# Half-width products in a gated-recurrence kernel: pairs of 64 keys by 64 queries, one in each half of TensorE's columns

## The chip, the cores and the metric

The kernel runs on one core of a Trainium2 chip. The metric is the device time of one execution in microseconds (us), lower is better. TensorE (PE) multiplies, VectorE (DVE) and ScalarE (ACT) work elementwise, GpSimd (POOL) does some elementwise work here and issues a few DMAs, SyncE (SP) issues most DMAs. A product on TensorE is two records in a trace: the load of the stationary operand (LDWEIGHTS, listed as engine PEld) and the matmul that streams the moving operand past it (MATMUL, listed as PE).

## The reference, cut to what matters

Two blocks follow each other. The first has a gated linear recurrence over 16 heads; this is what the change touches:

```python
def step(S, inp):                        # one chunk of 64 positions
    qc, kc, vc, gc = inp
    b = jnp.cumsum(gc, axis=-2)
    decay = jnp.exp(jnp.where(causal, b[..., :, None, :] - b[..., None, :, :], -jnp.inf))
    scores = jnp.einsum('bhtc,bhtsc,bhsc->bhts', qc, decay, kc)
    o = einsum('bhts,bhsv->bhtv', scores, vc) + einsum('bhtc,bhcv->bhtv', qc * jnp.exp(b), S)
    ...
```

It runs forward and backward over 256 context and 512 latent positions, head size 128, and its input is a projection of the normalised tokens to five streams a head (query, two gates, value, output gate). A Fourier mixer and a second block (two feed-forward layers and a token mixer) follow; nothing in them changes. All of it is in float32.

## The kernel before

**Weights.** Every large product is made as three (high by high, high by low, low by high) of operands cut into two parts of type fp32r; they are recorded under the helper `three` at L489. SyncE brings weights in blocks of 128 by 1024 into two buffers (`w_raw`), ACT makes `w_hi` (L1060), DVE makes `w_lo` (L1603).

**Heads.** `pe_head(i, j)` is TensorE's program of one trip: the projections (`project`) of head i, and between them the recurrence of head j = i - 1. It is written out once for the first head, as a loop over 15 trips, and once for the last head, where the place of the projections is taken by the start of the output product (`begin_output`). The order inside a trip is written by hand, in three rows that begin

```python
project(0, "a"); project(0, "b"); diagonal(); level(0)
project(1, "a"); level(1); turn_v_context(); project(1, "b"); level(2)
project(1, "c"); level(3); project(2, "a"); level(4); project(2, "b"); level(5)
project(2, "c"); level(6); project(3, "a"); turn_k(0); ...
```

**Scores by levels.** The scores of the 512 latent positions are needed only inside tiles of 128 (`tile(t)`, four tiles, `TT`); between tiles the recurrence carries a state. Inside a tile they come from a tree with 7 levels: at level l a block of 2^l keys meets the sibling block of 2^l queries. `K` and `Q` hold keys and queries of both directions; `merge(l)` on DVE (L1825) multiplies them by the decays of that level, in place; ACT copies the keys of the level in order of position to `K_now` (`weave`, L1215); TensorE multiplies them with the queries, which `woven` picks from the two directions' halves of `Q` by an access pattern of runs of 2^l (L663). `diagonal` (L650) multiplies the summed keys `ksum` with `q_st` for the pairs of a position with itself. Each of these eight steps makes four float32 products of 128 keys by 128 queries, contraction 128, into one bank of `ps` (bank 4 or 5), and of each product DVE takes by mask the places that the level owns (`place`, COPY_PREDICATED at L1804) into `ST`. At levels 0 to 5 and on the diagonal these places all lie in the two 64 by 64 squares on the tile's diagonal, at level 6 in the two squares off it.

**What starts what.** TensorE waits with `dve(l)` for the queries of level l, with `k_woven` for its keys, and with `gates_ready` for `ksum`; DVE waits for TensorE's products through `pe_scan`. After level 1 come two transposes (L642), after the levels transposes of `K` (L676), products of keys and values (L685), the output (L695 to L697) and the norm (L704). At the program's start, before the heads, `ada_raw` is multiplied with a stationary operand of only two columns, `csil` (L546); in between stands the mean of L528, with a stationary operand of 128 columns; then come 16 transposes of two rows (L554).

Of the kernel before, what the change touches and what calls it, by code (L numbers as in the profile page):

```python
# [31 lines left out]
P = 128  # L32
# [30 lines left out]
LEVELS = 7  # L63
BLK = KD * P
BF = 258
HALF_T = T // 2
FOLD = TT // 2


_sizes = [("c", 2 * KD), ("ada_b0", 16), ("gate_b", 16), ("ada_b1", 16), ("norm_g0", KD), ("norm_g1", KD),  # L70
# [71 lines left out]
def woven(t, at, size, n, first):  # L142

    wide = t.shape[2]
    step = n + (wide if first == 0 else -wide)
    return bass.AP(t, at + first * wide, [[2 * wide, P], [2 * n, size // (2 * n)], [step, 2], [1, n]])
# [22 lines left out]
def program(nc, wts, ada_in, gate_in, x_in, ctx_in, meta_in, vec_in, mask_in, ident_in, dft_in, chan_in, out):  # L171
    nblocks = wts.shape[0]
    with ExitStack() as top:
# [42 lines left out]
        q_st = h.take("q_st", [P, T])  # L216
# [4 lines left out]
        Q = h.take("Q", [P, 2, T])  # L221
        K = h.take("K", [P, 2, TA])
        K_now = h.take("K_now", [P, 2, T])
        ksum = h.take("ksum", [P, T])
# [17 lines left out]
        g_hi, g_lo = f.take("g_hi", [P, KD, T], F32R), f.take("g_lo", [P, KD, T], F32R)  # L242
        F_hi = f.take("F_hi", [P, FOLD, T], F32R)
        F_lo = f.take("F_lo", [P, FOLD, T], F32R)
        C_hi = f.take("C_hi", [P, 2, 2, 2, P], F32R)
# [7 lines left out]
        fgain, fgain_sq = q.take("fgain", [P, KD]), q.take("fgain_sq", [P, KD])  # L253
        F_raw, C_raw = f.take("F_raw", [P, FOLD, T]), f.take("C_raw", [P, 2, 2, 2, P])
        h_now, h_fold = f.take("h_now", [P, T]), f.take("h_fold", [P, T])
# [34 lines left out]
        ps = top.enter_context(nc.psum_tensor("ps", [P, 8, T], F32))  # L290
# [156 lines left out]
        def _(pool):  # L447
# [26 lines left out]
            pool.wait_ge(y_cut, HEADS)  # L474
            pool.dma_start(F_raw[:], dft_in[:, 0:FOLD]).then_inc(dft_in_s, 16)
            pool.dma_start(C_raw[:], chan_in).then_inc(chan_in_s, 16)
# [5 lines left out]
        def _(pe):  # L482
            st = Stream()

            def three(outs, whi, wlo, xhi, xlo, start, stop):

                for n, (w, x) in enumerate(((whi, xhi), (whi, xlo), (wlo, xhi))):
                    for o, xp in zip(outs, x):
                        last = nc.tensor.matmul(o, w, xp, start=start and n == 0,  # L489
                                                stop=stop and n == 2)  # L490
                return last
# [7 lines left out]
            def tiles(s, outs, xs, ks, start, stop, first=0):  # L499

                for n, k in enumerate(ks):
                    c = slice((first + n) * P, (first + n + 1) * P)
                    last = three(outs, w_hi[:, s, c], w_lo[:, s, c], *xs(k),
                                 start=start and n == 0, stop=stop and n == len(ks) - 1)
                return last
# [4 lines left out]
            def halved(hi, lo):  # L510
                return lambda k: ([hi[:, k, 0:HALF], hi[:, k, HALF:TM]],
                                  [lo[:, k, 0:HALF], lo[:, k, HALF:TM]])

            def bank2(b):
                return [ps[:, b, 0:HALF], ps[:, b + 1, 0:HALF]]
# [15 lines left out]
            def tile_cols(t):  # L531
                return slice(t * P, (t + 1) * P)
# [8 lines left out]
            for n, (raw_, a, b_) in enumerate(ADA_LOADS):  # L541
                pe.wait_ge(ada_loaded[n], 16)
                for k in range(KD):
                    if n == 1 and k == KD - 2:
                        mean(N0, T, st_sum[:, 0])
                    last = nc.tensor.matmul(ps[0:2, n], csil[:, k], raw_[:, :, k * P:(k + 1) * P],  # L546
                                            start=k == 0, stop=k == KD - 1)
# [5 lines left out]
            for m_ in range(16):  # L553
                last = nc.tensor.transpose(ps[:, 7, 2 * m_:2 * m_ + 2], ada_row[:, m_ // 4, tile_cols(m_ % 4)],  # L554
                                           ident[0:2, 0:2])
# [4 lines left out]
            def tile(t):  # L560
                return slice(t * P, (t + 1) * P)
# [8 lines left out]
            def pe_head(i, j):  # L570
# [49 lines left out]
                def dve(n):  # L620
                    pe.wait_ge(dve_scan, j * DVE_SCAN + n)
# [15 lines left out]
                def turn_v_context():  # L637
# [4 lines left out]
                        last = nc.tensor.transpose(ps[:, 6, tile(t)], v_st[:, tile(t)], ident[:])  # L642
                    last.then_inc(pe_scan, 1)

                def diagonal():
                    if j is None:
                        return
                    pe.wait_ge(gates_ready, j + 1)
                    for t in range(TT):
                        last = nc.tensor.matmul(ps[:, 4, tile(t)], ksum[:, tile(t)], q_st[:, tile(t)],  # L650
                                                start=True, stop=True)
                    last.then_inc(pe_scan, 1)

                def level(l):
                    if j is None:
                        return
                    if l == 0:
                        pe.wait_ge(act_scan, j * ACT_SCAN + 7)
                    else:
                        dve(l)  # L660
                    pe.wait_ge(k_woven, j * LEVELS + (l + 1))
                    for t in range(TT):
                        last = nc.tensor.matmul(ps[:, 5 - l % 2, tile(t)], K_now[:, l % 2, tile(t)],  # L663
                                                woven(Q, t * P, P, 2 ** l, 1), start=True, stop=True)
                    last.then_inc(pe_scan, 1)

                def steps(g_):
# [32 lines left out]
                def norm():  # L700
# [3 lines left out]
                    nc.tensor.matmul(ps[:, 5], ones_h[:], osq[:], start=True, stop=True).then_inc(pe_scan, 1)  # L704
# [4 lines that stand above are left out]
                project(2, "c"); level(6); project(3, "a"); turn_k(0); project(3, "b"); outer(0)  # L709
                turn_k(1); project(3, "c"); outer(1); turn_k(2); project(4, "a"); outer(2)  # L710
# [4 lines left out]

            st.enter(0, 6)
            pe_head(0, None)
            st.leave(1)
            with hinted(pe, 0, HEADS - 1) as j:
                st.enter(j, 6)  # L720
                pe_head(j + 1, j)
            st.leave(HEADS - 1)
            st.enter(0, 2 * EARLY)
            pe_head(None, HEADS - 1)
            st.leave(1)
            pe.wait_ge(kept_s, EARLY)
            for n in range(LATE):
                t = HEADS - LATE + n
                pe.wait_ge(y_cut, t + 1)
                for k in range(EARLY):  # L730
                    last = three([ps[:, k]], kept_hi[:, k, n * P:(n + 1) * P], kept_lo[:, k, n * P:(n + 1) * P],
                                 [y_hi[:, t]], [y_lo[:, t]], False, n == LATE - 1)
# [44 lines left out]
            def over_tokens(c):  # L777
# [4 lines left out]
                for t in range(TT):  # L782
                    part, m_ = divmod(t, FOLD)
                    o, at = ((ps[:, 6, 0:BF], slice(0, BF)), (ps[:, 7, 0:HALF_T], slice(HALF_T, T)))[part]
                    last = three([o], t_hi[:, tile(t)], t_lo[:, tile(t)],
                                 [F_hi[:, m_, at]], [F_lo[:, m_, at]], m_ == 0, m_ == FOLD - 1)
                last.then_inc(pe_ft, 1)
# [177 lines left out]
            with hinted(pe, 0, KD // 2) as i:  # L965
                st.enter(i, 14)
                for k in range(14):
# [13 lines left out]
                    for m_ in range(2):  # L981
                        last = tiles(s, bank2(4 + 2 * m_), halved(xr_hi, xr_lo), range(2), True, True, 2 * m_)
# [610 lines left out]
        def _(dve):  # L1593
            st = Stream()
            own = Own(dve, own_s["dve"])
            v = nc.vector
# [66 lines left out]
            v.memset(eps[:], EPS)  # L1663
            v.memset(tiny[:], 2.0 ** -100)
            v.memset(eps_sq[:], EPS * EPS)
            v.memset(zero[:], 0.0).then_inc(consts_set, 1)
            dve.wait_ge(vec_in_s, 16)
            lb = vec[:, VEC["lb"]:VEC["lb"] + 4 * HEADS].rearrange("p (n c) -> p n c", n=2)
# [945 lines left out]
```

## Time and profile before

| | us |
|---|---|
| median of 3 runs | 2518.79 (2518.48 to 2519.62) |
| profiled execution, its own time | 2521.25 |
| span of its trace, first to last instruction | 2518.5 |
| TensorE matmul busy | 2461.1 (98%) |
| TensorE weight load busy | 2147.0 (85%) |
| VectorE busy | 1633.3 (65%) |
| ScalarE busy | 993.6 (39%) |
| GpSimd busy | 120.3 (5%) |

The mean granted clock of TensorE is 0.992 of full speed. Busy shares add up over stages that have different limits. A matmul's recorded duration reaches beyond the moment at which the next one starts, so what one costs in a row of its kind is the distance between starts, or its share of a piece in the chain of work that ended last.

### The profile page before, as it was taken

How to read it: one execution, taken by the hardware profiler on the slowest of the kernel's cores; microseconds unless marked ns; L12 is line 12 of the kernel's file. 1: busy time of each engine (PE TensorE's matmuls, PEld its weight loads, DVE VectorE, ACT ScalarE, POOL GpSimd, SP SyncE). 2: the span in 40 equal slices, each digit the busy share in tenths (PEclk: the TensorE clock that was granted, in tenths of full speed). 3: DMA queues.
4: the chain of work that ended last, by engine and by line, in shares of the span. 5: the costliest groups of instructions: out<-in, count | busy, mean ns of one | idle time of the engine just before them, and what ended most of it. 6: DMA issues, size and time to landing. Idle time of an engine off the chain costs nothing.

```text
span 2518.5 us, 40380 instructions
## 1 busy us (share of the span) xinstructions
PE 2461.1 (98%) x14398; PEld 2147.0 (85%) x14398; DVE 1633.3 (65%) x2378; ACT 993.6 (39%) x1338; POOL 120.3 (5%) x138
## 2 busy tenths in 40 slices
PE   7999999999999998999999999989999999999998
PEld 2888888888888886888899999979999878888886
DVE  7567777777777775445555343468999975444346
ACT  4334444444444433333345222235455554322223
POOL 0011211111111100000000000000000000000000
PEclk9999999999999998999999999999999999999999
DMA  6212212122121232222222222222222222222222
GB/s 239 78 64 75 75 67 75 58 76 82 67 67 64 78 126 75 83 76 83 85 92 91 88 88 92 92 84 92 100 97 94 100 84 97 95 92 92 99 92 100
DMA packets 61983, 223.90 MB, mean 89 GB/s; under 512 B 6736, under 2 KB 8784, under 8 KB 61552
## 3 DMA queue, kind: packets, MB, share of 16 engines
q1 hardware_dynamic: 58992, 211.08, 24.7%
q0 software_dynamic: 2944, 12.19, 1.4%
q8 instruction: 29, 0.48, 0.1%
q14 instruction: 18, 0.15, 0.0%
HBM read 221.15 MB, written 2.10 MB: 89 GB/s over the span
## 4 chain that ended last, share of the span: by engine, by line
PE 93%; DVE 4%; ACT 1%; issue 1%; DMA 1%; ACTq 0%; DVEq 0%; SPq 0%
PE ps L489 81%; PE ps L663 4%; PE ps L685 1%; PE ps L546 1%; DMA ada_raw<-in_ada_weights_dram 1%; PE ps L676 1%; PE ps L704 1%; PE ps L650 1%; PE ps L695 1%; PE ps L696 1%; PE ps L697 1%; ACT w_hi L1060 1%; DVE w_lo L1603 1%; PE ps L633 0%; DVE n_sq L1622 0%
## 5 line engine op out<-in xcount | busy, mean ns | idle before, releaser
L1060 ACT ACTIVATE w_hi<-w_raw 128x1024 fp32r<-128x1024 f32 (+1 forms) x360 | 377.8, 1049 | 922.5 <-PE ps L489 913.7
L1603 DVE TENSOR_TENSOR w_lo<-w_raw,w_hi 128x1024 fp32r<-128x1024 f32 (+1 forms) x360 | 435.3, 1209 | 214.4 <-ACT w_hi L1060 212.2
L489 PE MATMUL ps<-n_hi,w_hi 128*128 128x512 f32 (+1 forms) x992 | 320.5, 355 | 11.9 <-DVE n_lo L1630 8.5
L489 PE MATMUL ps<-n_lo,w_hi 128*128 128x512 f32 (+1 forms) x992 | 319.6, 354 | 0.0
L489 PE MATMUL ps<-n_hi,w_lo 128*128 128x512 f32 (+1 forms) x992 | 318.0, 352 | 0.0
L489 PE MATMUL ps<-h_hi,w_hi 128*128 128x512 f32 x640 | 266.5, 416 | 4.8 <-DVE h_lo L1735 3.1
L489 PE MATMUL ps<-h_hi,w_lo 128*128 128x512 f32 x640 | 251.2, 393 | 0.0
L489 PE MATMUL ps<-h_lo,w_hi 128*128 128x512 f32 x640 | 250.4, 391 | 0.0
L489 PEld LDWEIGHTS ps<-n_hi,w_hi 128*128 128x128 f32 x992 | 174.5, 189 | 45.4 <-issue 11.0
L489 PEld LDWEIGHTS ps<-n_hi,w_lo 128*128 128x128 f32 x992 | 174.6, 189 | 25.9
L489 PEld LDWEIGHTS ps<-n_lo,w_hi 128*128 128x128 f32 x992 | 174.4, 189 | 26.1 <-issue 0.2
L489 PE MATMUL ps<-y_lo,w_hi 128*128 128x512 f32 x504 | 179.1, 397 | 6.6 <-DVE y_lo L1630 6.6
L489 PEld LDWEIGHTS ps<-h_hi,w_hi 128*128 128x128 f32 x640 | 121.0, 189 | 32.8 <-issue 10.0
L489 PE MATMUL ps<-hid_hi,w_hi 128*128 128x264 f32 (+2 forms) x540 | 143.4, 318 | 0.7 <-DVE w_lo L1603 0.7
L489 PE MATMUL ps<-xg_hi,w_hi 128*128 128x264 f32 x704 | 143.9, 285 | 0.0
L489 PE MATMUL ps<-xg_lo,w_hi 128*128 128x264 f32 x704 | 143.8, 285 | 0.0
L489 PE MATMUL ps<-xg_hi,w_lo 128*128 128x264 f32 x704 | 143.6, 285 | 0.0
L489 PE MATMUL ps<-hid_lo,w_hi 128*128 128x264 f32 (+2 forms) x540 | 143.4, 319 | 0.0
L489 PEld LDWEIGHTS ps<-h_hi,w_lo 128*128 128x128 f32 x640 | 120.4, 188 | 26.8
L489 PE MATMUL ps<-hid_hi,w_lo 128*128 128x264 f32 (+2 forms) x540 | 142.9, 318 | 0.0
L489 PEld LDWEIGHTS ps<-h_lo,w_hi 128*128 128x128 f32 x640 | 121.3, 190 | 22.1
L1215 ACT ACTIVATE K_now<-K 128x512 f32<-128x512 f32 x112 | 75.4, 673 | 154.5 <-DVE K L1825 138.4
(367 smaller groups left out, 4963.8 us busy)
## 6 DMA issues: line engine op xcount, KB each, us to landing
w_raw<-in_weights_dram SPq DMA_DIRECT2D x376, 512.0 KB, 3.3
ada_raw<-in_ada_weights_dram SPq DMA_DIRECT2D x4, 2048.0 KB, 22.4
gate_raw<-in_gate_weights_dram POOLq DMA_DIRECT2D x16, 512.0 KB, 3.6
x<-in_x_dram SPq DMA_DIRECT2D x1, 2048.0 KB, 14.6
x<-in_x_dram POOLq DMA_DIRECT2D x1, 2048.0 KB, 9.9
out_dram<-fin SPq DMA_DIRECT2D x16, 128.0 KB, 1.9
xc<-in_ctx_dram SPq DMA_DIRECT2D x1, 1024.0 KB, 21.2
masks<-in_masks_dram POOLq DMA_DIRECT2D x1, 512.0 KB, 4.8
```

Of the source, the lines that this page charges most:

```text
L489: last = nc.tensor.matmul(o, w, xp, start=start and n == 0, stop=stop and n == 2)
L546: last = nc.tensor.matmul(ps[0:2, n], csil[:, k], raw_[:, :, k * P:(k + 1) * P], start=k == 0, stop=k == KD - 1)
L650: last = nc.tensor.matmul(ps[:, 4, tile(t)], ksum[:, tile(t)], q_st[:, tile(t)], start=True, stop=True)
L663: last = nc.tensor.matmul(ps[:, 5 - l % 2, tile(t)], K_now[:, l % 2, tile(t)], woven(Q, t * P, P, 2 ** l, 1), start=True, stop=True)
L676: last = nc.tensor.transpose(ps[:, 6, tile(x)], K[:, d, tile(ORDER[d][n])], ident[:])
L685: last = nc.tensor.matmul(ps[:, 4 + g_ % 2, tile(x)], KT[:, x], V[:, ORDER[d][n]], start=True, stop=True)
L695: nc.tensor.matmul(o, V[:, CT + t], ST[:, t], start=True, stop=False)
L696: nc.tensor.matmul(o, states[:, 1 + t, 0], Q[:, 0, tile(t)], start=False, stop=False)
L697: last = nc.tensor.matmul(o, states[:, 4 - t, 1], Q[:, 1, tile(t)], start=False, stop=True)
L1060: run(w_hi[:, s, 0:n], w_raw[:, s, 0:n], ACT.Copy).then_inc(hi_ready[s], 1)
L1215: run(K_now[:, l % 2], woven(K, TC, T, 2 ** l, 0), ACT.Copy).then_inc(k_woven, 1)
L1603: tt(w_lo[:, s, 0:n], w_raw[:, s, 0:n], w_hi[:, s, 0:n].bitcast(F32), ALU.subtract).then_inc(lo_ready[s], 1)
```

## The change

A product of 128 keys by 128 queries becomes two of 64 by 64. The keys of a half tile are the stationary operand (64 columns), and the result goes to partitions 0 to 63 of `ps` for the first half of the keys and to 64 to 127 for the second, so each product stands in one half of the array's columns. On the diagonal and at levels 0 to 5 the queries are those of the same half; at level 6 those of the other half, which lie in one direction's part of `Q` and need no weaving. The squares of the bank that are not written any more are never taken by a mask, but are still read; the two banks are set to zero once at the start.

```diff
+HALF_TILE = P // 2
...
+                def half_tiles(t):
+                    return [slice(t * P + x * HALF_TILE, t * P + (x + 1) * HALF_TILE) for x in range(2)]
+
                 def diagonal():
                     if j is None:
                         return
                     pe.wait_ge(gates_ready, j + 1)
                     for t in range(TT):
-                        last = nc.tensor.matmul(ps[:, 4, tile(t)], ksum[:, tile(t)], q_st[:, tile(t)],
-                                                start=True, stop=True)
+                        for x, c in enumerate(half_tiles(t)):
+                            last = nc.tensor.matmul(ps[x * HALF_TILE:(x + 1) * HALF_TILE, 4, c], ksum[:, c], q_st[:, c],
+                                                    start=True, stop=True)
                     last.then_inc(pe_scan, 1)
 
                 def level(l):
...
                     for t in range(TT):
-                        last = nc.tensor.matmul(ps[:, 5 - l % 2, tile(t)], K_now[:, l % 2, tile(t)],
-                                                woven(Q, t * P, P, 2 ** l, 1), start=True, stop=True)
+                        cs = half_tiles(t)
+                        for x, keys in enumerate(cs):
+
+                            at = cs[1 - x] if l == LEVELS - 1 else keys
+                            queries = Q[:, x, at] if l == LEVELS - 1 else woven(Q, at.start, HALF_TILE, 2 ** l, 1)
+                            last = nc.tensor.matmul(ps[x * HALF_TILE:(x + 1) * HALF_TILE, 5 - l % 2, at],
+                                                    K_now[:, l % 2, keys], queries, start=True, stop=True)
                     last.then_inc(pe_scan, 1)
...
             v.memset(eps_sq[:], EPS * EPS)
+            v.memset(ps[:, 4:6], 0.0)
             v.memset(zero[:], 0.0).then_inc(consts_set, 1)
```

Waits and signals stay as they are. On TensorE, in the loop over the heads, this stood from the diagonal through level 1 before (output by keys and queries; a product here is one instruction, which the trace shows as two loads and two matmuls):

```order
L489 MATMUL ps<-h_hi,w_lo 128x512
L650 MATMUL ps<-q_st,ksum 128x128 x4
L658 ISA
L661 REGISTER_ALU
L663 MATMUL ps<-Q,K_now 128x128 x4
L572 REGISTER_ALU
L489 MATMUL ps<-h_hi,w_hi 128x512
...
L663 MATMUL ps<-Q,K_now 128x128 x4
L624 ISA
L642 MATMUL ps<-ident,v_st 128x128 x2
```

And this stands there now:

```order
L490 MATMUL ps<-h_hi,w_lo 128x512
L657 MATMUL ps<-q_st,ksum 64x64 x8
L665 ISA
L668 REGISTER_ALU
L675 MATMUL ps<-Q,K_now 64x64 x8
L573 REGISTER_ALU
L490 MATMUL ps<-h_hi,w_hi 128x512
...
L675 MATMUL ps<-Q,K_now 64x64 x8
L625 ISA
L643 MATMUL ps<-ident,v_st 128x128 x2
```

Nothing has moved: each run of four products of 128 by 128 has become a run of eight of 64 by 64, between neighbours of full width. Levels 2 to 6 each stand alone between two projections in the same way. On DVE, this is the start of the program before:

```order
L1665 MEMSET eps_sq 128x1
L1666 MEMSET zero 128x1
L1669 TENSOR_TENSOR lbt<-vec 128x32
L1670 TENSOR_TENSOR lbt<-vec,lbt 128x64
L1672 TENSOR_SCALAR rgc<-vec 128x8
```

and now:

```order
L1677 MEMSET eps_sq 128x1
L1678 MEMSET ps 128x1024
L1679 MEMSET zero 128x1
L1682 TENSOR_TENSOR lbt<-vec 128x32
L1683 TENSOR_TENSOR lbt<-vec,lbt 128x64
```

One instruction, the zeroing of the two banks, has come in ahead of the signal `consts_set`.

## Rows read from the trace of the kernel before

**Rows 1.** Page, part 1: busy us, share of the span, instructions.

```profile
PE 2461.1 (98%) x14398; PEld 2147.0 (85%) x14398; DVE 1633.3 (65%) x2378; ACT 993.6 (39%) x1338; POOL 120.3 (5%) x138
```

**Rows 2.** Windows: busy us of each engine in one trip of the heads.

```profile
core 0: us, PE busy (x) PEld busy (x) DVE busy (x) ACT busy (x) POOL busy (x), PEclk, DMA share, GB/s
252.59:304.55 51.96, 51.96 (x324) 46.11 (x323) 39.51 (x63) 22.97 (x35) 7.39 (x9) 1.00 0.21 71
```

**Rows 3.** Chain that ended last, in order: start, us, work; one trip.

```profile
304.71 0.89 PE ps L650 x8
305.60 1.33 PE ps L663 x8
...
309.68 1.12 PE ps L663 x8
...
313.76 0.89 PE ps L663 x8
```

**Rows 4.** The same chain: level 1 in the second and the last head.

```profile
153.92 0.96 PE ps L663 x8
881.20 0.96 PE ps L663 x8
```

**Rows 5.** Timeline around level 3: start, us, engine, line, work.

```profile
317.25 0.28 PE L489 MATMUL ps<-hc_hi,w_lo 128*128 128x256 f32 x1
317.25 0.98 PEld L663 LDWEIGHTS ps<-Q,K_now 128*128 128x128 f32 x8
317.37 1.06 PE L663 MATMUL ps<-Q,K_now 128*128 128x128 f32 x8
```

**Rows 6.** Line L663, all of it: duration ns, min/median/max.

```profile
L663 PEld LDWEIGHTS ps<-Q,K_now x896: 186/192/198, 97.8 to 900.1; 128*128 128x128 f32 x180
L663 PE MATMUL ps<-Q,K_now x896: 270/275/383, 97.9 to 900.3; 128*128 128x128 f32 x180
```

**Rows 7.** Timeline of the start: two-column (L546) and full-width (L528) products.

```profile
26.27 0.59 PE L546 MATMUL ps<-ada_raw,csil 128*2 128x512 f32 x1
26.79 0.70 PE L528 MATMUL ps<-st_sum,ones_d 128*128 128x512 f32 x1
26.79 0.30 PEld L528 LDWEIGHTS ps<-st_sum,ones_d 128*128 128x128 f32 x2 [0.86 <-issue]
27.32 0.59 PE L528 MATMUL ps<-st_sum,ones_d 128*128 128x512 f32 x1
27.85 0.59 PE L546 MATMUL ps<-ada_raw,csil 128*2 128x512 f32 x1
30.28 13.89 PE L546 MATMUL ps<-ada_raw,csil 128*2 128x512 f32 x32
```

**Rows 8.** The 16 transposes of two rows: durations ns of the loads; timeline.

```profile
L554 PEld LDWEIGHTS ps<-ident,ada_row x16: 133/137/141, 44.9 to 45.9; 2*128 2x128 f32 x16
...
44.91 1.08 PEld L554 LDWEIGHTS ps<-ident,ada_row 2*128 2x128 f32 x16 [1.67 <-issue]
44.95 1.14 PE L554 MATMUL ps<-ident,ada_row 2*128 2x2 f32 x16 [0.77 <-ACT ada_row L1113]
```

**Rows 9.** Timeline ahead of level 1: DVE, then level 1's first load.

```profile
304.25 1.22 DVE L1603 TENSOR_TENSOR w_lo<-w_raw,w_hi 128x1024 fp32r<-128x1024 f32 x1
305.74 1.87 DVE L1825 TENSOR_TENSOR K<-K,f_st 128x768 f32<-128x768 f32 x1 [0.27 <-PE ps L650]
...
308.40 1.03 DVE L1825 TENSOR_TENSOR Q<-Q,f_st 128x512 f32<-128x512 f32 x1
309.56 1.02 PEld L663 LDWEIGHTS ps<-Q,K_now 128*128 128x128 f32 x8 [0.31 <-issue]
```

**Rows 10.** Timeline of the program's start on DVE and ahead of TensorE.

```profile
2.88 0.17 DVE L1662 MEMSET ones_h<- 128x128 f32 x1
11.60 2.72 PE L546 MATMUL ps<-ada_raw,csil 128*2 128x512 f32 x3 [11.60 <-DMA ada_raw<-in_ada_weights_dram]
17.07 0.43 DVE L1617 COPY st_sum<-st_tmp 128x512 f32<-128x512 f32 x1 [6.99 <-ACT st_tmp L1087]
```

## The prediction

> **What bounds the kernel now.** The page first: TensorE is busy 98% of the span, DVE 65% [rows 1]. The windows of one trip of the heads say it more sharply: in a trip of 51.96 us TensorE is busy for all 51.96, at full granted clock, DVE for 39.51 [rows 2]. So in the heads, where all of the change lies, a microsecond of TensorE's time is a microsecond of the kernel, as long as DVE keeps up. The chain of work that ended last prices each piece: the diagonal 0.89 us, level 0 1.33, level 1 1.12, any other level 0.89 [rows 3]. In the 16 heads there are 80 pieces of 0.89 from levels 2 to 6. Level 1 takes 1.12 (1.11 to 1.14) in the 13 heads from the third to the fifteenth, and 0.96 in the other three [rows 3, 4].
>
> What is in 0.89 us? Four products are eight passes, each a load of 128 columns and a stream of 128 queries. The matmuls start (1.06 - 0.275)/7 = 0.112 us apart, and the loads (0.98 - 0.19)/7 = 0.113 [rows 5, 6]. So a pass costs 0.111 (0.89/8), and the loads alone would fill the time as well as the streams do: each load lies under the stream before it. Level 0 costs 1.33/8 = 0.167 a pass; its queries alternate between the two halves of `Q` at every element.
>
> **What the change does to a run of products.** The passes of a diagonal or a level go from 8 to 16, each with half the columns to load and half the queries to stream. If cost follows columns, a pass falls from 0.111 to 0.056 and a run stays at 16 x 0.056 = 0.89; level 0 stays at 1.33. Halving the columns of both operands saves a factor of four in array work, but twice the passes take back a factor of two, and the other factor comes only if the two halves of the array work at the same time. The trace of before has no such pair. The least that a load with its matmul takes in it, back to back, is in the 16 transposes of two rows and two streamed columns: (1.08 - 0.14)/15 = 0.063 for the loads and (1.14 - 0.19)/15 = 0.063 for the matmuls [rows 8]. There hardly anything is streamed. I bound a half-width pass from below by 0.030 (two halves in full parallel, half of 0.056, rounded up) and from above by 0.063, and take 0.060 for the likeliest case: halves one after the other at 0.056, plus a little, towards the one row with such short work. A run then costs 0.96 instead of 0.89, so +0.07.
>
> The diagonal and levels 1 to 6 are 7 x 16 = 112 runs: 112 x 0.07 = +7.8 us (0 to +13.4 with 0.056 to 0.063). Level 0: +0.04 in 16 heads, +0.6.
>
> The Trainium skill, "TensorEngine Tiling (Array Packing)", section Key Properties, states that tiles operate independently and that different tiles can load and multiply in parallel; by it alone a pass would be near 0.030 and a run near 0.48. No row of this trace shows two tiles at work together, so it makes the second rival below and not the sum.
>
> **What it adds at the edges of a run.** This is the larger term. The trace shows TensorE changing between a narrow stationary operand and a full one, at the start of the program. Products with two stationary columns follow each other at (13.89 - 0.59)/31 = 0.429 us. From the last of them to the first full-width product it is 26.79 - 26.27 = 0.52 instead, so 0.09 more; and the full-width load starts only then, at 26.79, not under the stream before, so its 0.11 is exposed too: the next matmul follows after 27.32 - 26.79 = 0.53 = 0.43 + 0.10. Back to two columns it is again 27.85 - 27.32 = 0.53 instead of 0.43: 0.10 more, with a load too short to see [rows 7]. The second such place, around 29.65, shows the same gaps. So TensorE runs empty before it changes between a narrow and a full operand, and the first load after the change is not covered. In the heads no width changes today, and every first load lies under the stream before it [rows 5].
>
> In the changed kernel every run is fenced by full-width work on both sides. Diagonal and level 0 adjoin and make one narrow stretch, levels 1 to 6 one each: 7 stretches a head, 112 in all. Entering costs 0.09 and an exposed load of 64 columns, 0.056; leaving costs 0.09 and an exposed load of 128 columns, 0.11. That is 0.35 us a stretch, 112 x 0.35 = +39.2 us. From below: nothing, if 64 columns do not count as another shape of the array. From above: the tail of a matmul beyond its stream, 0.275 - 0.11 = 0.16 [rows 6], in place of each 0.09, so 0.49 a stretch and +55 us.
>
> The Trainium skill, same page and section, says that changing the tiling mode, not just the tile, drains TensorE. By that rule both edges of every stretch pay and the two halves inside one do not; the trace agrees for two columns against 128, with the 0.09 and 0.10 above.
>
> **What goes away.** Level 1 waits for its queries: DVE ends them at 308.40 + 1.03 = 309.43, and the load starts at 309.56 [rows 9]. That wait is the 1.12 - 0.89 = 0.23 in 13 heads. With a diagonal and level 0 that take 0.07 + 0.04 + 0.35 = 0.46 longer, TensorE comes late enough to find the queries there, though DVE's start also waits for the diagonal and slips by some 0.2 (entering plus 0.07). The wait mostly goes: 13 x 0.23 = -3.0 us.
>
> **What costs nothing.** The new MEMSET of 1024 columns. The 128-column one takes 0.17 with its fixed part, so this one takes at most 8 x 0.17 = 1.4 us, at about 3 us on DVE. TensorE's first work waits for a DMA until 11.60, and DVE later sits idle 6.99 us before 17.07 [rows 10]; both cover it. Uncovered it would be 1.4 us. DMAs, waits and signals are as before, and DVE, with 12 us to spare in a trip, follows a slower TensorE.
>
> **Sum.** +39.2 + 7.8 + 0.6 - 3.0 = +44.6 us. The profiled execution took 2521.25, so 2565.9 for its like; against the median of the runs, 2518.79 + 44.6 = **2563** us, 1.8% slower. A difference of 0.2% (5 us) is about what a measurement of this kernel can tell from none.
>
> **Rivals.**
>
> 1. *Slower by the edges, as above.* For it: both edges are in the trace, and loads fill a run today. Own range 2545 to 2580: the edges at 0.28 to 0.40 and the pass at 0.056 to 0.063. Chance 0.60. With the full tail at the edges instead it is 2518.8 + 55 + 5 = 2579 or more; chance 0.07.
>
> 2. *The halves work in parallel, and the edges are paid* (the other side). A pass averages 0.030, a run 0.48, so levels 1 to 6 save 0.41 each and pay 0.35: -0.06 x 96 = -6 us. Diagonal and level 0 together go from 2.22 to about 0.48 + 0.70 + 0.35 = 1.53, but most of that is not gained: level 1's queries are ready only 3.7 us after DVE starts on `K`, DVE starts when the diagonal is done, and it cannot start before 304.25 + 1.22 = 305.47, 0.27 ahead of today [rows 9]. So -0.25 x 16 = -4 us, and the wait at level 1 grows. 2509 us. It decides as soon as an average pass falls below (0.89 - 0.35)/16 = 0.034 us. For it: nothing forbids it in the trace, and the placing in two halves asks for it. Against: in the heads' float32 products a load starts no sooner than 0.11 after the load before it [rows 5], so one path that serves both halves in turn is enough to undo the gain. Chance 0.17.
>
> 3. *Parallel halves and free edges*: 96 x -0.41 = -39, -4 for the first stretch: 2476 us. Against it stand rows 7. Chance 0.05.
>
> 4. *In turn, with free edges*: +8.4 - 3.0: 2524 us, hardly to be told from before. Chance 0.08. The remaining 0.03 is for a loss beyond 2590, if a half-width pass has a floor of its own above 0.063.
>
> **How the numbers follow.** The likeliest case gives 2563. The range 2506 to 2580 leaves out the third rival and the slowest tail, some 0.13 in all. Faster by over 0.2%: the third rival whole and most of the second, whose 2509 lies 10 us under before: 0.05 + 0.14 = 0.19. Within 0.2%: part of what is left of the second, 0.02, and most of the fourth, 0.06, together 0.08. Slower: the rest, 0.73.
>
> **What the changed profile would show.** Step by step: (a) the chain gives the diagonal and levels 1 to 6 pieces of about 1.2 to 1.3 us, for 16 passes each; if they come near 0.8, the halves ran in parallel. (b) Starts of half-width matmuls about 0.056 to 0.063 apart inside a run; if they come in twos with hardly a gap, or at 0.03, rival 2 or 3 holds. (c) The first load of a run starts some 0.09 after the stream before it ended, and not under it; the same for the first projection load after a run. If not, the edges are free. (d) No idle stretch at level 1; a larger one speaks for rival 2. (e) A trip of 51.96 us becomes one of about 54.7. (f) TensorE stays the engine that is never idle; DVE's busy time in a trip stays near 39.5. The prediction falls with (b) or (c), which are two independent measurements that the trace of before makes only for other shapes.

## The result, and the profile after

The changed kernel takes 2504.64 us (median of 4 runs, 2503.56 to 2505.99) against 2519.12 for the kernel before. The ratio is 0.9943, with a 95% interval of 0.993 to 0.9955: it is faster by 0.57%, where 1.8% slower was forecast.

The page of the changed kernel, part 1, in the columns of [rows 1]:

```profile
PE 2441.0 (98%) x15422; PEld 2093.5 (84%) x15422; DVE 1636.7 (65%) x2379; ACT 995.0 (40%) x1338; POOL 120.3 (5%) x138
```

TensorE has 1024 more records of each kind, which is 128 runs of 8 more passes, and is busy for 20 us less. The windows of one trip, from one diagonal to the next, answer to [rows 2]:

```profile
core 0: us, PE busy (x) PEld busy (x) DVE busy (x) ACT busy (x) POOL busy (x), PEclk, DMA share, GB/s
299.28:350.46 51.18, 50.75 (x388) 42.79 (x387) 39.69 (x63) 23.07 (x35) 7.35 (x9) 1.00 0.23 72
```

A trip lasts 51.18 us instead of 51.96, so 0.78 less; and TensorE is idle for 0.43 of it, where it had not been idle at all. The chain that ended last shows both (start, us, work; "issue" is time in which nothing in the profile was waited for; it answers to [rows 3]):

```profile
299.35 0.64 PE ps L657 x16
...
300.11 0.11 DVE K L1838
300.22 1.96 issue
302.18 0.76 DVE ST L1817
...
303.05 1.04 DVE Q L1838
304.10 0.12 issue
304.21 0.71 PE ps L675 x16
...
308.05 0.61 PE ps L675 x16
308.66 3.07 PE ps L490 x24
311.73 0.62 PE ps L675 x16
...
350.53 0.64 PE ps L657 x16
```

Level 2 is the piece at 308.05: 0.61 for 16 passes. The piece behind it, 24 matmuls of a projection, has grown from 2.88 to 3.07, as it carries the exposed load on the way back. So the fair measure of a level is the distance from the start of level 2 to that of level 3: 311.73 - 308.05 = 3.68. Before, level 2 starts at 313.76 [rows 3] and level 3, in the same chain, here:

```profile
314.65 2.88 PE ps L489 x24
317.53 0.89 PE ps L663 x8
```

That is 3.77 (3.76 in the next trip), so 2.87 or 2.88 of it are the projection, and a level costs 0.81 instead of 0.89. The second thing to see is the top of the fence: between the diagonal (299.35) and level 1 (304.21) the chain has left TensorE and runs over DVE, its multiplication of `K`, its masked copy and its multiplication of `Q`. Level 1 now waits for its queries. The timeline of the same stretch shows what stands behind the 0.11 of `K` and the 1.96 of issue:

```profile
299.02 0.87 ACT L1227 ACTIVATE K_now<-K 128x512 f32<-128x512 f32 x1 [0.77 <-DVE ksum L1813]
299.07 2.38 POOL L461 TENSOR_TENSOR f_tree<-f_st 128x768 f32<-128x768 f32 x1 [43.25 <-DVE ksum L1813]
299.28 0.69 PE L657 MATMUL ps<-q_st,ksum 128*64 128x64 f32 x16
299.94 0.69 PEld L675 LDWEIGHTS ps<-Q,K_now 128*64 128x64 f32 x16
300.11 2.15 DVE L1838 TENSOR_TENSOR K<-K,f_st 128x768 f32<-128x768 f32 x1
```

The multiplication of `K` takes 2.15 us here and 1.87 before [rows 9], and the other multiplications of `K`, at the later levels, mostly 0.94 to 0.96. Before, GpSimd's multiplication of `f_st` stood here:

```profile
304.43 2.38 POOL L460 TENSOR_TENSOR f_tree<-f_st 128x768 f32<-128x768 f32 x1 [44.06 <-DVE ksum L1800]
```

It ends at 306.80, and `K` at 307.61; now they end at 301.45 and 302.26. So in both kernels this `K` ends 0.81 us after GpSimd, however early it starts. Now it starts 1.04 after GpSimd instead of 1.31, so 0.27 earlier, and takes 0.28 longer. Level 1's queries are finished 5.00 after GpSimd's start before [rows 9] and 5.01 now. A second, smaller wait lies ahead of level 0: ACT writes its keys until 299.89, its first load starts at 299.94, and from the diagonal's start that is 0.66 where 16 passes need 0.47.

The timeline around level 4 shows a stretch and its edges (start, us, engine, line, work):

```profile
314.90 0.39 PE L490 MATMUL ps<-h_hi,w_lo 128*128 128x512 f32 x1
315.22 0.55 PEld L675 LDWEIGHTS ps<-Q,K_now 128*64 128x64 f32 x16 [0.35 <-issue]
315.22 0.69 PE L675 MATMUL ps<-Q,K_now 128*64 128x64 f32 x16
315.84 0.19 PEld L490 LDWEIGHTS ps<-h_hi,w_hi 128*128 128x128 f32 x1
315.84 0.50 PE L490 MATMUL ps<-h_hi,w_hi 128*128 128x512 f32 x1
...
316.17 0.39 PE L490 MATMUL ps<-h_lo,w_hi 128*128 128x512 f32 x1
```

The first narrow load comes 0.32 after the last full-width matmul began, where 0.23 is the usual distance: 0.09 of nothing. The 16 matmuls, each recorded with 0.22, start within 0.69 - 0.22 = 0.47, so 0.031 apart on average. Record by record they come in twos: the two halves of a tile start 0.007 apart, loads and matmuls alike, and the twos follow each other every 0.058. And the first two full-width matmuls behind are 0.33 apart, not 0.23: the exposed load of 128 columns.

### The profile page after: what moved, and what is told of

The parts are those of the page before. It is cut to its first block, busy times and chain, and to the rows that moved or that the text cites. A ratio compares the mean times of both kernels' runs of the same rounds, so it can differ in the third digit from the quotient of the medians.

```text
span 2502.7 us, 42429 instructions
## 1 busy us (share of the span) xinstructions
PE 2441.0 (98%) x15422; PEld 2093.5 (84%) x15422; DVE 1636.7 (65%) x2379; ACT 995.0 (40%) x1338; POOL 120.3 (5%) x138
## 4 chain that ended last, share of the span: by engine, by line
PE 91%; DVE 5%; issue 2%; ACT 1%; DMA 1%; DVEq 0%; ACTq 0%; SPq 0%
PE ps L490 81%; PE ps L675 2%; PE ps L697 1%; PE ps L547 1%; PE ps L688 1%; DMA ada_raw<-in_ada_weights_dram 1%; PE ps L716 1%; DVE Q L1838 1%; PE ps L708 1%; PE ps L709 1%; PE ps L707 1%; ACT w_hi L1072 1%; DVE w_lo L1615 1%; DVE ST L1817 0%; PE ps L657 0%
```

## The experiments

Each edit is to the changed kernel unless said otherwise. The third column is the yardstick from above, the distance between the starts of levels 2 and 3 in one trip's chain; 2.87 of it are the projection. Before, it is 3.76 or 3.77 by the trip.

| kernel | us (median) | level 2 to level 3 | a level | ratio to before, 95% |
|---|---|---|---|---|
| before | 2519.12 | 3.76 | 0.89 | |
| changed | 2504.64 | 3.68 | 0.81 | 0.993 to 0.9955 |
| one half (e1) | 2557.68 | 4.14 | 1.27 | 1.0124 to 1.0183 |
| half by half (e2) | 2531.23 | 3.96 | 1.09 | 1.0028 to 1.0073 |
| two tiles (e5) | 2526.51 | 3.90 | 1.03 | 1.0019 to 1.0046 |
| levels 1 to 6 only (e3) | 2506.82 | 3.68 | 0.81 | 0.9941 to 0.9971 |
| diagonal and level 0 only (e4) | 2517.96 | 3.77 | 0.89 | 0.9988 to 1.0007 |
| later level 1 (e6) | 2499.22 | 3.69 | 0.81 | 0.9912 to 0.9939 |
| before, later level 1 (e7) | 2515.50 | 3.77 | 0.89 | 0.998 to 0.9998 |
| quarters (e8) | 2483.65 | 3.46 | 0.59 | 0.9846 to 0.9879 |
| quarters, six tiles (e9) | 2480.16 | 3.44 | 0.57 | 0.9832 to 0.9864 |
| halves, six tiles (e10) | 2497.92 | 3.67 | 0.80 | 0.9903 to 0.9936 |

**Do the halves work together, or is a narrow pass just cheap?**

```diff
-ps[x * HALF_TILE:(x + 1) * HALF_TILE, 4, c]
+ps[0:HALF_TILE, 4, c]
...
-ps[x * HALF_TILE:(x + 1) * HALF_TILE, 5 - l % 2, at]
+ps[0:HALF_TILE, 5 - l % 2, at]
```

DVE's masked copy takes partitions 0 to 63 only, and the rest of `ST` is zeroed once.

> The changed kernel, with both products of a tile sent to partitions 0 to 63, so that both stand in the same half of the columns (the scores of the second half's keys are left out, and ST is zero there). Theory A, two halves work at the same time only because they are different halves: a pass goes from 0.029 to 0.056 to 0.063 us, a run of 16 from 0.47 to 0.9 to 1.0, level 0 from 0.67 to 1.33, and the wait ahead of level 1 goes: 112 x 0.45 + 16 x 0.66 - 14 x 0.5 = +54, about 2558 us, near what was predicted. Rival B, a half-width pass simply costs about 0.03 wherever it stands: 2505 us, starts as dense as now.

It took 2557.68 us, 1.54% slower than before and 53 slower than the changed kernel. The chain of this kernel from a diagonal on:

```profile
367.75 1.07 PE ps L657 x16
368.83 1.33 PE ps L675 x16
...
373.12 1.10 PE ps L675 x16
...
377.35 1.08 PE ps L675 x16
378.42 3.07 PE ps L490 x24
381.49 0.55 PE ps L675 x7
```

The same instructions with the same shapes, in one half of the columns: a diagonal or a level takes 1.07 to 1.10 instead of 0.61 to 0.71, level 0 is back at 1.33, and no wait stands ahead of level 1. Theory A holds. The overlap of the two halves is worth 1.27 - 0.81 = 0.46 a level. Its passes start 0.058 apart, one by one. This kernel is the one that was forecast: without the overlap, half-width products are slower than full ones. The half of the columns is picked here by the output partitions, so no run tells apart whether the one or the other must differ.

**How far ahead does TensorE reach for the idle half?**

```diff
-for t in range(TT):
-    for x, keys in enumerate(half_tiles(t)):
+for x in range(2):
+    for t in range(TT):
```

> The changed kernel, with the loops swapped: first the four products in the lower half of the columns, then the four in the upper half. If the overlap is between neighbours in the program only, the halves work one after the other: about 2555 us, starts 0.056 apart. If TensorE reaches eight passes ahead for work of the idle half: 2505 us, as now.

It took 2531.23 us, between the two expectations. Its chain:

```profile
368.59 0.90 PE ps L676 x16
369.49 3.06 PE ps L490 x24
372.55 0.49 PE ps L676 x6
```

A level costs 1.09, so 0.18 less than in one half, and a pass in turn takes 0.057 (below): about three of the eight upper passes were hidden under the lower ones, not none and not all. The single records of this level agree: the first load of the upper half starts at 368.808, together with the sixth of the lower half (368.807), when two more of the lower half are still to come. That TensorE looks only some three passes ahead is the reading that fits; only this length of run was tried.

**What do the edges cost?**

```diff
+if l > 0 and t >= 2:
+    last = nc.tensor.matmul(ps[:, 5 - l % 2, tile(t)], K_now[:, l % 2, tile(t)],
+                            woven(Q, t * P, P, 2 ** l, 1), start=True, stop=True)
+    continue
```

> Diagonal and level 0 as changed; at levels 1 to 6 only the first two of four tiles in half-width pairs, the other two at full width. Theory, the edges of a narrow stretch cost 0.3 to 0.35 us whatever its length, and a tile saves 0.11: a level costs 0.89 + 0.32 - 0.22 = 1.0 instead of 0.81, 96 x 0.19 = +18, about 2523 us, slower than both kernels. Rival, no price at the edges, and a tile saves only 0.02 (a quarter of the 0.08 that a level saves): 96 x 0.04 = +4, about 2509 us.

It took 2526.51 us. Its level 2 in the chain, four narrow products and two full ones:

```profile
366.71 0.38 PE ps L679 x8
367.10 0.64 PE ps L671 x4
367.74 2.87 PE ps L490 x24
370.61 0.38 PE ps L679 x8
```

A level costs 1.03. Three kernels now give three equations, with E for both edges and h for a tile in halves side by side, s for one in one half, and 0.222 for a full tile (0.89/4): E + 4h = 0.81, E + 2h + 0.444 = 1.03, E + 4s = 1.27. So h = 0.112, E = 0.36, s = 0.228, which is 0.057 a pass in turn and 0.028 a pass side by side. Three equations for three unknowns leave nothing over to check them by; the changed kernel's trace does it, at its level 4: on the way in 0.09 of nothing and a first pass longer by 0.05, on the way out 0.09 and 0.11, together 0.34. The rival without edges is out: half of the pairing costs 22 us more than all of it.

**Which part gave the gain?**

> Half-width pairs at levels 1 to 6 alone, diagonal and level 0 at full width as before. Theory: each level saves 0.08 us net of its edges, 96 x 0.08 = -8, with level 1's wait much as before: about 2511 us. Rival, the gain comes from the diagonal and level 0: 2519 us, as before.

> Half-width pairs on the diagonal and at level 0 alone, levels 1 to 6 at full width. Theory: this stretch saves about 0.7 us of TensorE's time a head, of which level 1's queries, which are no more than 0.3 us earlier, let through about 0.3: 16 x 0.3 = -5, about 2514 us, with an idle stretch of about 0.5 us ahead of level 1. Rival, nothing holds level 1 back and all of it is gained: 2508 us.

Levels 1 to 6 alone (diagonal and level 0 as before): 2506.82 us. Diagonal and level 0 alone: 2517.96, with an interval that holds no change. So the levels gave nearly all, more than I expected, and the first stretch nothing. The chain of the second kernel says how its saving was lost:

```profile
354.21 0.64 PE ps L657 x16
...
357.90 1.05 DVE Q L1842
358.95 0.12 issue
359.07 1.22 PE ps L671 x8
...
363.26 0.89 PE ps L671 x8
```

From the start of the diagonal to that of level 2 it takes 363.26 - 354.21 = 9.05 us; before, 313.76 - 304.71 = 9.05 too [rows 3]. TensorE is faster and stands in front of the same queries. They come no earlier: in this kernel too the first multiplication of `K` starts earlier and takes 2.14 instead of 1.87, ending 0.82 after GpSimd's multiplication of `f_st`. In all twelve traces it ends 0.81 or 0.82 after it in every head from the second on. GpSimd's multiplication starts when `ksum` is ready, and the diagonal does not enter into it. Why DVE is held up is open, as no run moved GpSimd's work. With levels 1 to 6 alone the same distance is shorter:

```profile
351.72 0.89 PE ps L656 x8
...
360.46 0.62 PE ps L678 x16
```

That is 8.74, so 0.31 less. The run e7 below, the kernel before without its wait, parts this in two: it takes 8.90, so 0.15 of the 9.05 was the old wait, and the other 0.16 is level 1's own saving. In the changed kernel the distance is 8.70.

**Is the wait ahead of level 1 a real loss?**

```diff
 if part == "a":
-    tiles(s, [ps[:, a]], xs, range(4), True, False)
+    tiles(s, [ps[:, a]], xs, range(5 if k == 1 else 4), True, False)
 elif part == "b":
-    last = tiles(k % 2, [ps[:, a]], xs, range(4, 8), False, True, 4)
+    last = tiles(k % 2, [ps[:, a]], xs, range(5 if k == 1 else 4, 8), False, True, 5 if k == 1 else 4)
```

> The changed kernel, with the fifth of the eight tiles of projection 1 moved from behind level 1 to ahead of it (three matmuls, 0.69 us of TensorE's work), so that TensorE comes later to level 1. Theory, 0.5 us a head are lost in the wait for level 1's queries in 14 heads: the wait goes, -7, about 2497.5 us. Rival, the wait only moves to level 2 or the diagonal: 2504.5 us.

> The kernel before with the same move of three matmuls ahead of level 1. The wait of 0.23 us in 13 heads goes: -3, about 2516 us. If it moves elsewhere: 2519 us.

The changed kernel with this takes 2499.22 us, 5.4 less; the kernel before takes 2515.50, 2.9 less than its own neighbour runs (2518.39). The chain of e7:

```profile
354.52 0.89 PE ps L651 x8
...
360.17 0.96 PE ps L664 x8
...
363.42 0.89 PE ps L664 x8
```

Level 1 costs 0.96 here with nothing to wait for, not 0.89: its passes start 0.120 apart. So the old wait was 1.12 - 0.96 = 0.16 us, and a trip has become 0.16 shorter, 51.80 instead of 51.96. In 13 heads that is 2.1 us, which the interval of e7 (0.5 to 5) can't tell from the expected 3. The chain of the changed kernel with the move:

```profile
349.05 0.61 PE ps L658 x16
349.66 0.86 PE ps L676 x16
350.52 3.64 PE ps L490 x15
354.16 0.65 PE ps L676 x16
...
357.25 0.62 PE ps L676 x16
```

The chain stays on TensorE, and the diagonal lies 8.20 ahead of level 2: the first stretch's saving of 0.5 us a trip appears only now. The 0.86 of level 0 still holds the wait for its keys: in the first two heads of this run, where they are ready in time, it is 0.67. That is 0.19 in 14 heads, 2.7 us, which a move of tiles behind level 0 can't give back. With six tiles ahead instead of five nothing more is to be had at level 1:

> e6_later_level1 with six tiles ahead of level 1 instead of five. The wait is gone with five already, so nothing is left to gain: 2499 us, or 1 to 2 us more if level 2 now waits for its keys.

2497.92 us (2496.63 to 2499.49), which overlaps the runs with five (2498.96 to 2499.83).

**Does it go on with quarters?** At levels 0 to 4 and on the diagonal the needed squares are 32 by 32.

```diff
+if l < LEVELS - 2:
+    for x in range(4):
+        c = slice(t * P + x * 32, t * P + (x + 1) * 32)
+        last = nc.tensor.matmul(ps[x * 32:(x + 1) * 32, 5 - l % 2, c], K_now[:, l % 2, c],
+                                woven(Q, c.start, 32, 2 ** l, 1), start=True, stop=True)
+    continue
```

> The kernel with the later level 1 (e6_later_level1, 2499.2 us), with the diagonal and levels 0 to 4 in four products of 32 keys by 32 queries a tile, each in a quarter of the columns; levels 5 and 6 stay in halves. If four quarters work at the same time as two halves do, a run of these falls from 0.47 to about 0.25: 80 x 0.22 + 16 x 0.35 = -23, of which up to 5 come back as a wait for level 1's queries: about 2480 us. If TensorE reaches only some three passes ahead, as in e2_half_by_half, only two to three quarters overlap: a run of about 0.35, about 2490 us. Rival, a pass with its load has a floor of about 0.03 us: 32 passes take 0.96, 80 x 0.5 = +40, about 2540 us.

> e8_quarters with six of projection 1's eight tiles ahead of level 1 instead of five. If level 1 waits again in e8_quarters, and level 2 has room, it is 2 to 4 us faster than that; if level 2 then waits for its keys, 2.4 us behind level 1, no faster.

2483.65 us with five tiles ahead of level 1, 2480.16 with six: 1.5% faster than before (0.9832 to 0.9864) and 1% faster than the change studied here. The timeline of the second at its level 3:

```profile
352.68 0.35 PEld L675 LDWEIGHTS ps<-Q,K_now 128*32 128x32 f32 x32
352.68 0.46 PE L675 MATMUL ps<-Q,K_now 128*32 128x32 f32 x32
353.07 0.19 PEld L490 LDWEIGHTS ps<-h_hi,w_hi 128*128 128x128 f32 x1
353.07 0.50 PE L490 MATMUL ps<-h_hi,w_hi 128*128 128x512 f32 x1
```

32 passes start within 0.46 less the duration of the last, about 0.22, so some 0.24: 0.008 apart. Record by record the matmuls start in fours, 0.007 apart, and the fours follow each other every 0.032: all four quarters work together. A row of passes has no floor of 0.03, but inside one quarter a pass takes 0.032, where one in a half takes 0.058. The result does not speak against a reach of three passes. The next pass of the same quarter is the fourth in the program, so three ahead are enough to keep four quarters at work, and the expectation of 2490 us took the limit in e2 for a tighter one than it is. The level costs 0.57, of which 0.36 would be the edges if they are the same as for halves: the run has nearly gone and its edges stay. With five tiles the chain has 0.09 of issue ahead of level 1, which the sixth removes.

## Why the prediction was wrong

**The step that failed** is the price of a half-width pass: "halves one after the other at 0.056, plus a little", 0.060. Measured side by side it is 0.028 a pass, and 0.057 only when both products are sent to one half (e1). The sum built on it, +7.8 and +0.6 us, should have been: 16 passes at 0.028 give 0.45 instead of 0.89, so 112 x -0.44 = -49.3 us, and level 0 gives 16 x (0.67 - 1.33) = -10.6. With the edges, 112 x 0.36 = +40.3, that is -19.6; e6 and e10, in which level 1 does not wait, came to -19.2 and -21.0 against their neighbour runs, and the changed kernel to -14.5 with the wait. I took the transposes of two rows [rows 8], 0.063 for a load and a matmul, as the row "with such short work". They bound nothing: quarters start every 0.008. Those transposes all stand in one place of the array, one after the other, and could not show what two places do. The row was of the right size and of the wrong kind, and I used it to choose between two ends, 0.030 and 0.063, of which the first was right.

By the rule of the Trainium skill, "TensorEngine Tiling (Array Packing)", section Key Properties, that different tiles can load and multiply in parallel, a run was to come to 0.48; the trace agrees, with 0.47 between the first and the last start.

**The edges** were right in place and size. Foreseen was 0.35 a stretch for entering, leaving and two exposed loads, from two products in the program's start [rows 7]; the three equations give 0.36, and the 0.09 of nothing stands in the timeline on the way in. The Trainium skill, "TensorEngine Tiling (Array Packing)", section Key Properties, has the rule that a change of the tiling mode drains TensorE; the trace agrees, with this 0.09.

**The wait ahead of level 1** was forecast to go, as a result of the wrong pass price, and its size was wrong too: -3.0 us took level 1 at 0.89 without a wait, and with the 0.96 of e7 it is 13 x 0.16 = 2.1. It grew instead: by the windows TensorE is idle 0.43 us of a trip, and the trip is 51.18 us, not 54.7. The second rival had it, "the wait at level 1 grows", and also that most of the first stretch's saving would be lost to it; e4 shows all of it lost, where 0.25 a head was expected to come through. The step that failed there is "level 1's queries are ready only 3.7 us after DVE starts on `K`": DVE did start 0.27 earlier, and the queries took 3.97. The price of `K` was taken as fixed, and it depends on how much of GpSimd's multiplication it meets. Rival 2's 2509 us was 4 too high: levels 2 to 6 save 0.08 to 0.09 each where it had 0.06, and level 1 saves 0.16 of its own and the 0.15 of its old wait (e3, e7) where it had 0.06.

**The zeroing** of two banks took 0.91 us on DVE at 3.28 us (1.4 at most was foreseen), ahead of TensorE's first product at 9.88, and costs nothing.

**The sum as measured.** A trip is 0.78 shorter: 0.35 between the diagonal and level 2 (9.05 to 8.70), and 0.43 from there to the first transposes of `K`, through levels 2 to 6 (18.49 to 18.06). The first matmul behind the recurrence starts at 927.05 before and at 911.94 now, 15.1 earlier. Of these, 1.8 are not the change's: the chain's DMA of `ada_raw` at the start takes 19.16 us in the one execution and 17.39 in the other. That leaves 13.3 of the 14.5 us between the medians; the rest lies within what single executions differ by.

**The chances.** The case that came true, halves side by side with edges paid, had 0.17, the one forecast 0.60. The evidence for parallel halves was absent, not negative, and the low chance rested on that. What was held against them, one path that loads both halves in turn, is out: the loads of the two halves start 0.007 apart.

## What to carry to other kernels

A product that needs only blocks on the diagonal of its tile can be cut to those blocks, if each goes to its own group of output partitions, neighbours in the program belong to different groups, and the whole stretch is long enough to pay 0.36 us for leaving and re-entering full width; a level cut to quarters gained four times as much as one cut to halves (0.32 against 0.08 us). When a stretch of the bounding engine gets shorter, look at once at which wait follows it: here moving three matmuls, without touching the change, was worth a further 5 us. When a multiplication on DVE slows down as it starts earlier, look at what GpSimd does at that time. And when the trace has no row for a mode, a row of another mode is no bound: give both ends their chance, or measure.

## What the runs showed of the hardware

Identical float32 products of 64 by 64 cost 0.057 us a pass in one half of the columns and 0.028 spread over two; those of 32 by 32 over four quarters start 0.008 us apart, which is 0.032 inside one quarter. TensorE ran work of the idle half ahead of the other half's queue, but in e2 only for about three of eight passes. Changing between full-width and narrow stationary operands left TensorE empty for 0.09 us each way, for 2 columns [rows 7] as for 64, and the first load behind it was exposed (0.11 for 128 columns, 0.05 for 64). A full-width product with queries in runs of two elements cost 0.120 us a pass (e7, level 1), in runs of one 0.167, otherwise 0.111. DVE's first multiplication of `K` in a head ended 0.81 us after a GpSimd multiplication that overlapped it, and took 1.67 to 2.2 us by how long they overlapped (0.85 us in e1, 1.41 in e8), where those that meet none take 0.94 to 0.96; the cause was not tested.
